# Latent attention in one DiT-like step: value products of head pairs in two column halves, four slots, maxima two items ahead

## The chip, the cores and the metric

The kernel runs on one core of a Trainium2 chip. The metric is the device time of one execution in microseconds; three runs give the time before. A NeuronCore has TensorE (PE, matrix products into PSUM; its weight loads are listed apart as PEld), VectorE (DVE), ScalarE (ACT), GpSimd (POOL) and SyncE (SP), each with an instruction stream of its own that runs in order, tied together by semaphores.

## What is computed

One inference step of a two-layer backbone over 128 context tokens and 512 latent tokens. Layer 0 has differential attention, layer 1 multi-head latent attention (MLA), and each layer ends in an expert-retrieval mixer, which takes most of the time. The change touches only the attention proper of layer 1, which is, cut to what matters:

```python
MLA_HEADS = 16; MLA_QK_DIM = 96; MLA_V_DIM = 64      # SEQ 128, DEC_SEQ 512, PAST_LEN 128

def attend(q, k, v, mix):                            # in blocks of Q_BLOCK = 128 queries
    scale = Dq ** -0.5
    def one(qblk):
        s = jnp.einsum('bqhd,bkhd->bhqk', qblk, k, preferred_element_type=jnp.float32) * scale
        w = mix(jax.nn.softmax(s, axis=-1))
        return jnp.einsum('bhqk,bkhd->bqhd', w.astype(v.dtype), v)

op = mla_out(qp, kp, vp, mla_wo[j])                               # 128 context queries, 128 context keys
os_ = mla_out(qs, jnp.concatenate([k_lat, k_ctx], axis=1),        # 512 latent queries,
              jnp.concatenate([v_lat, v_ctx], axis=1), mla_wo[j]) # 512 latent + 128 cached keys
```

with `mix` the identity. All is float32.

## The kernel before

The kernel is one program of blocks with a barrier of all engines between them; in a block, each engine has its instructions written out by hand, and semaphores count finished instructions. Layer 1 goes: norm, `mla_compress`, then for each of two groups of eight heads `mla_heads` (queries, keys, values of the group) and `mla_attention`, then the output product. `mla_attention` runs twice.

It works through 40 items in a call: a head (eight) and a block of 128 queries (five, `qb` 0 to 3 latent, 4 context). A latent item has 640 keys, a context item 128: four large items and one small for each head. The steps of an item are:

- scores on TensorE (lines 1110 and 1111, in a small item 1113): 128 queries by 512 and 128 keys, contraction over 96, into two PSUM banks of `ps`, 0 and 1 or 2 and 3 in turn;
- maximum on VectorE (line 1154) and its scaling by the query's norm (line 1157), into `small`;
- exponential on ScalarE (line 1183) from PSUM into a slot of `pr` (three slots), with the row sum, which comes as a short instruction of its own;
- reciprocal of the sum (line 1163) and the weights, `pr` times it, in place, on VectorE (line 1166);
- transposes of `pr` on TensorE (line 1123), one for each 128 keys, into banks 4 and 5, and their copy to `pT` (two slots) on ScalarE (line 1192);
- value product on TensorE (line 1134): 128 columns of `V`, which are two heads, as stationary operand, `pT` as moving one, into bank 6 or 7. Half of the result belongs to the other head and is thrown away: the copy of the result on ScalarE (line 1198) takes 64 partitions.

A float32 product is two passes of TensorE, with a weight load each, so that a value product of five matmuls shows as x10 in the trace; a transpose is one.

The order is software-pipelined by hand. TensorE in step w: scores of w, value product of w - 3, transposes of w - 2. ScalarE: exponential of w, copy of w - 2, result of w - 3. VectorE: maximum of w + 1, then weights of w. All VectorE instructions count up one semaphore, `ma_w`, so that a wait for some step of it is a wait for all before it. Before its transposes TensorE waits for the weights of that item:

```python
pe.wait_ge(sem(n_ + "w"), 4 * (o + w + 1) + (2 if w + 1 < len(items) else 0))
```

`diff_attention` of layer 0 has the same shape, with two score products for each item, one on rows 0 to 63 of the array and one on rows 64 to 127 (lines 486 and 487), value product on line 509.

Of the kernel before, what the change touches and what calls it, by code (L numbers as in the profile page):

```python
# [21 lines left out]
ALU = mybir.AluOpType  # L22
ACT = mybir.ActivationFunctionType
AX = mybir.AxisListType.X

P = 128
# [34 lines left out]
def mixed(nc, cst, inp, outs, g_dram, x_dram):  # L61
# [32 lines left out]
    def bank2(b, n=T, p=P):  # L94

        return ps[0:p, b:b + 2, :].rearrange("p a n -> p (a n)")[:, 0:n]
# [987 lines left out]

    def mla_attention(g, qT, kT, V, rsq, oT, pr, pT):

        items = [(h, qb) for h in range(GH) for qb in range(TB)]
        n_ = "ma_"
        o = g * len(items)

        def width(qb):
            return T if qb < 4 else TP

        with nc.Block() as block:
            @block.sync
            def _(sp):
                if g == 0:
                    for name in sorted(sems):
                        if name.startswith("mh_"):
                            sp.sem_clear(sems[name])  # L1100

            @block.tensor
            def _(pe):
                def scores(w):
                    h, qb = items[w]
                    q, k, b = qT[0:DQ, h, qb * P:(qb + 1) * P], kT[0:DQ, h, :], 2 * (w % 2)
                    if w >= 2:
                        pe.wait_ge(sem(n_ + "exp"), o + w - 1)
                    if qb < 4:
                        pe.matmul(ps[:, b, :], q, k[:, 0:TS], start=True, stop=True)  # L1110
                        mm = pe.matmul(ps[:, b + 1, 0:TC], q, k[:, T:TK], start=True, stop=True)
                    else:
                        mm = pe.matmul(ps[:, b, 0:TP], q, k[:, TS:T], start=True, stop=True)
                    mm.then_inc(sem(n_ + "s"), 1)

                def turns(w):
                    h, qb = items[w]
                    blocks = (0, 1, 2, 3, 5) if qb < 4 else (4,)
                    pe.wait_ge(sem(n_ + "w"), 4 * (o + w + 1) + (2 if w + 1 < len(items) else 0))
                    if w >= 1:  # L1120
                        pe.wait_ge(sem(n_ + "pT"), o + w)
                    for k in range(len(blocks)):
                        mm = pe.transpose(bank2(4)[:, k * P:(k + 1) * P], pr[:, w % 3, 0, k * P:(k + 1) * P], ident)
                    mm.then_inc(sem(n_ + "t"), 1)

                def values(w):
                    h, qb = items[w]
                    blocks = (0, 1, 2, 3, 5) if qb < 4 else (4,)
                    pe.wait_ge(sem(n_ + "pT"), o + w + 1)
                    if w >= 2:  # L1130
                        pe.wait_ge(sem(n_ + "o"), o + w - 1)
                    for k, kb in enumerate(blocks):

                        mm = pe.matmul(ps[:, 6 + w % 2, 0:P], V[:, kb, (h // 2) * P:(h // 2 + 1) * P],
                                       pT[:, w % 2, k * P:(k + 1) * P], start=k == 0, stop=k == len(blocks) - 1)
                    mm.then_inc(sem(n_ + "pv"), 1)

                for w in range(len(items) + 3):
                    if w < len(items):
                        scores(w)  # L1140
                    if w >= 3:
                        values(w - 3)
                    if 2 <= w < len(items) + 2:
                        turns(w - 2)

            @block.vector
            def _(v):
                s = sem(n_ + "w")

                def maxima(w):  # L1150
                    n = width(items[w][1])
                    z = small[:, 16 * (w % 2):16 * (w % 2) + 16]
                    v.wait_ge(sem(n_ + "s"), o + w + 1)
                    v.tensor_reduce(z[:, 0:1], bank2(2 * (w % 2), n), AX, ALU.max).then_inc(s, 1)
                    v.wait_ge(s, 4 * o + (1 if w == 0 else 4 * w - 1))
                    h, qb = items[w]
                    v.tensor_scalar(z[:, 2:3], z[:, 0:1], rsq[:, 1, qb, h:h + 1], None, ALU.mult).then_inc(s, 1)

                def weights(w):
                    n = width(items[w][1])  # L1160
                    z = small[:, 16 * (w % 2):16 * (w % 2) + 16]
                    v.wait_ge(sem(n_ + "exp"), o + w + 1)
                    v.reciprocal(z[:, 6:7], z[:, 4:5]).then_inc(s, 1)
                    v.wait_ge(s, 4 * (o + w) + 3 + (2 if w + 1 < len(items) else 0))
                    p0 = pr[:, w % 3, 0, 0:n]
                    v.tensor_scalar(p0, p0, z[:, 6:7], None, ALU.mult).then_inc(s, 1)

                maxima(0)
                for w in range(len(items)):
                    if w + 1 < len(items):  # L1170
                        maxima(w + 1)
                    weights(w)

            @block.scalar
            def _(act):
                def exps(w):
                    h, qb = items[w]
                    n = width(qb)
                    z = small[:, 16 * (w % 2):16 * (w % 2) + 16]
                    if w >= 3:  # L1180
                        act.wait_ge(sem(n_ + "t"), o + w - 2)
                    act.wait_ge(sem(n_ + "w"), 4 * o + (2 if w == 0 else 4 * w))
                    act.activation(pr[:, w % 3, 0, 0:n], bank2(2 * (w % 2), n), ACT.Exp, bias=z[:, 2:3],
                                   scale=rsq[:, 2, qb, h:h + 1], accum_out=z[:, 4:5]).then_inc(sem(n_ + "exp"), 1)

                def copies(w):
                    h, qb = items[w]
                    n = width(qb)
                    act.wait_ge(sem(n_ + "t"), o + w + 1)
                    if w >= 2:  # L1190
                        act.wait_ge(sem(n_ + "pv"), o + w - 1)
                    act.copy(pT[:, w % 2, 0:n], bank2(4, n)).then_inc(sem(n_ + "pT"), 1)

                def results(w):
                    h, qb = items[w]
                    act.wait_ge(sem(n_ + "pv"), o + w + 1)
                    r = 64 * (h % 2)
                    act.copy(oT[r:r + 64, (g * GH + h) // 2, qb * P:(qb + 1) * P], ps[r:r + 64, 6 + w % 2, 0:P])\
                       .then_inc(sem(n_ + "o"), 1)

                for w in range(len(items) + 3):
                    if w < len(items):
                        exps(w)
                    if 2 <= w < len(items) + 2:
                        copies(w - 2)
                    if w >= 3:
                        results(w - 3)
# [676 lines left out]
    with es:  # L1884
# [20 lines left out]
        with ExitStack() as st:  # L1905
# [12 lines left out]
            with ExitStack() as sa:  # L1918
                cqT = sb(sa, "cqT", [P, 4, T])
                ckvT = sb(sa, "ckvT", [P, 2, TK])  # L1920
                kpeT, kpe_sq, kpe_rot = (sb(sa, name, [DR, TK]) for name in ("kpeT", "kpe_sq", "kpe_rot"))
                cq_ms = sb(sa, "cq_ms", [P, T])
                cos, sin = sb(sa, "cos_mla", [P, TK]), sb(sa, "sin_mla", [P, TK])
                with ExitStack() as s2:
                    mla_compress(ring, cqT, ckvT, kpeT, kpe_sq, kpe_rot, cq_ms, cos, sin, sb(s2, "scr_c", [P, 6, T]),
                                 sb(s2, "abuf_c", [P, 2, 2048]), sb(s2, "acc_c", [P, 2, 2, 256]))
                qT, kT = sb(sa, "qTm", [P, GH, T]), sb(sa, "kTm", [P, GH, TK])
                V = sb(sa, "Vm", [P, 6, GH * DV])
                for g in range(2):
                    with ExitStack() as s2:  # L1930
                        mla_heads(g, ring, indT, cqT, ckvT, kpe_sq, kpe_rot, cq_ms, qT, kT, V, rsq, cos, sin,
                                  sb(s2, f"scr_m{g}", [16, 2, TK]), sb(s2, f"xk{g}", [P, 2, TK]), hT[:, 4:6, :], hT[:, 6:8, :])
                    with ExitStack() as s2:
                        mla_attention(g, qT, kT, V, rsq, hT, sb(s2, f"pr_m{g}", [P, 3, 1, T]), sb(s2, f"pT_m{g}", [P, 2, T]))
            with ExitStack() as s2:
                out_product(1, ring, hT, J_WO1, range(J_PQ[1], J_PQ[1] + 3), sb(s2, "oh1", [P, DC, T], F32R),
                            sb(s2, "ol1", [P, DC, T], F32R), sb(s2, "woh1", [P, 2, DC, P], F32R),
# [155 lines left out]
```

## Time and profile before

| | us |
|---|---|
| runs | 4040.15, 4044.76, 4044.55 |
| median | 4044.55 |
| profiled execution, span of its instructions | 4043.5 |
| first call of `mla_attention` in it | 2219.65 to 2335.54, 115.89 |
| second call | 2420.90 to 2536.80, 115.90 |

The profiled execution has no time of its own beside its span, from the first to the last instruction; it is 1.05 us below the median. A profile gives for each instruction its start and duration; rows of the timeline merge neighbours of one line (xN), and what stands in brackets is how long the engine was idle before it and who released it. "PE" durations of matmuls include the pipeline's drain, so that starts, not durations, tell the rate: the distance from one weight load to that of the next step is what a step costs TensorE.

### The profile page before, as it was taken

Reading aid. Unit: us, or ns where it says so; the run is one execution under the profiler, and the core shown is the slowest. Engines: PE = TensorE matmul, PEld = TensorE weight load, DVE = VectorE, ACT = ScalarE, POOL = GpSimd, SP = SyncE. Lnnn points to the kernel's source line nnn. Section 1 sums busy time; section 2 is a strip of 40 time slices with the busy share of each in tenths; the row PEclk is TensorE's granted clock in tenths of the full one; section 3 lists DMA queues with packets and bytes.
Section 4 is the critical chain, followed back from the end, with each engine's and each line's share of the span. In section 5 each row is a group of like instructions: output and inputs, shape, how many; then the busy total and the mean of one; then the engine's idle time right before and its main releaser. Section 6 shows DMA issues by size and latency. Waiting matters only on the chain. (4 is left out here: it accounts for less than half of the span.)

```text
span 4043.5 us, 55694 instructions
## 1 busy us (share of the span) xinstructions
PE 3793.5 (94%) x20589; PEld 3188.6 (79%) x20589; DVE 3269.8 (81%) x6832; ACT 1769.0 (44%) x2928; POOL 988.0 (24%) x796
## 2 busy tenths in 40 slices
PE   6999999978999999999989898897789999999999
PEld 3555789677999999999854646896779999999998
DVE  2755648987999999999863525389979999999998
ACT  2324622185444444444423545322854444444443
POOL 0000000074333333333200000000743333333332
PEclk8999989999999999999989999898999999999999
DMA  6320020269999999999741010200799999999997
GB/s 238 136 94 11 22 89 37 98 174 361 420 419 414 405 403 404 404 404 406 312 177 43 1 42 1 109 37 22 185 375 420 417 412 407 405 405 405 405 406 300
DMA packets 268125, 1033.69 MB, mean 256 GB/s; under 512 B 147056, under 2 KB 150064, under 8 KB 159920
## 3 DMA queue, kind: packets, MB, share of 16 engines
q0 software_dynamic: 77184, 562.07, 34.7%
q1 hardware_dynamic: 190672, 468.07, 30.4%
q8 instruction: 164, 2.69, 0.3%
q14 instruction: 105, 0.86, 0.1%
HBM read 970.69 MB, written 59.39 MB: 255 GB/s over the span
## 5 line engine op out<-in xcount | busy, mean ns | idle before, releaser
L1637 POOL DMA_INDIRECT gbuf<-in_uv,rows x340 | 514.5, 1513 | 866.3 <-DVE hT L1821 796.5
L1429 POOL TENSOR_SCALAR pqT<-iota,selT 128x128 f32<-128x128 f32 x256 | 203.4, 809 | 1337.4 <-ACT selT L1371 1300.9
L1821 DVE SCALAR_TENSOR_TENSOR hT<-gbuf,act,hT 128x1024 f32<-128x1024 f32 x336 | 416.9, 1282 | 6.0
L1806 DVE SCALAR_TENSOR_TENSOR gbuf<-gbuf,ht 128x1024 f32<-128x1024 f32 x340 | 402.3, 1220 | 10.7 <-DMA gbuf<-in_uv,rows 10.7
L1637 POOL DMA_INDIRECT xT<-in_uv,rows x172 | 256.9, 1493 | 471.0 <-DVE hT L1821 392.9
L1653 PE MATMUL ps<-h1h,U1h 128*128 128x384 f32 x1024 | 344.5, 336 | 7.7 <-DVE U1l L1780 7.6
L1653 PE MATMUL ps<-h0h,U0h 128*128 128x384 f32 x1024 | 344.7, 337 | 5.1 <-DVE U0l L1780 5.1
L1653 PE MATMUL ps<-h0h,U0l 128*128 128x384 f32 x1024 | 344.2, 336 | 0.0
L1653 PE MATMUL ps<-h0l,U0h 128*128 128x384 f32 x1024 | 343.9, 336 | 0.0
L1653 PE MATMUL ps<-h1h,U1l 128*128 128x384 f32 x1024 | 343.9, 336 | 0.0
L1653 PE MATMUL ps<-h1l,U1h 128*128 128x384 f32 x1024 | 343.5, 335 | 0.0
L1726 ACT ACTIVATE ring<-ps 128x384 f32<-128x384 f32 x256 | 125.9, 492 | 379.0 <-PE ps L1653 378.9
L1736 ACT ACTIVATE act<-act 128x2 f32<-128x2 f32 x256 | 51.8, 202 | 457.1 <-DVE gbuf L1806 300.3
L1318 PE MATMUL ps<-pqT,w 128*128 128x128 f32 x1536 | 192.1, 284 | 50.8 <-DVE w L1562 36.1
L1268 PE MATMUL ps<-hT,ring 128*128 128x128 f32 x1920 | 231.7, 281 | 6.1 <-ACT hT L258 4.5
L1268 PEld LDWEIGHTS ps<-hT,ring 128*128 128x128 f32 x1920 | 224.3, 196 | 10.7 <-ACT hT L258 5.7
L1318 PEld LDWEIGHTS ps<-pqT,w 128*128 128x128 f32 x1536 | 181.7, 197 | 61.4 <-DVE w L1562 31.7
L1806 DVE SCALAR_TENSOR_TENSOR xT<-xT,ht 128x1024 f32<-128x1024 f32 x172 | 203.7, 1220 | 9.8 <-DMA xT<-in_uv,rows 9.8
L1821 DVE SCALAR_TENSOR_TENSOR hT<-xT,act,hT 128x1024 f32<-128x1024 f32 x168 | 208.4, 1282 | 3.0
L1653 PEld LDWEIGHTS ps<-h1h,U1h 128*128 128x128 f32 x1024 | 193.0, 189 | 11.1 <-DVE U1l L1780 8.7
L1653 PEld LDWEIGHTS ps<-h0h,U0h 128*128 128x128 f32 x1024 | 193.3, 189 | 8.2 <-DVE U0l L1780 5.8
L101 PE MATMUL ps<-hT,ring 128*128 128x512 f32 (+1 forms) x368 | 195.1, 613 | 4.5 <-ACT hT L258 4.5
(379 smaller groups left out, 9053.6 us busy)
## 6 DMA issues: line engine op xcount, KB each, us to landing
ring<-in_u SPq DMA_DIRECT2D x128, 1024.0 KB, 13.4
ring<-in_v SPq DMA_DIRECT2D x128, 1024.0 KB, 9.4
ring<-in_wts SPq DMA_DIRECT2D x26, 2048.0 KB, 8.3
gates<-ring SPq DMA_DIRECT2D x32, 1536.0 KB, 8.5
ring<-gates SPq DMA_DIRECT2D x64, 768.0 KB, 16.4
abuf<-in_ada_mid POOLq DMA_DIRECT2D x16, 1024.0 KB, 5.1
xT<-in_ada_late SPq DMA_DIRECT2D x16, 1024.0 KB, 4.8
abuf_c<-in_ada_late POOLq DMA_DIRECT2D x8, 1024.0 KB, 5.1
```

The costliest lines, as they stand in the source:

```text
L101: e.matmul(out[:, 0:512], lhsT, rhs[:, 0:512], start=start, stop=stop)
L1268: mm = pe.matmul(ps[:, 5 + n % 3, q * P:(q + 1) * P], w[:, dc, q * P:(q + 1) * P], hT[:, dc, tb * P:(tb + 1) * P], start=dc == 0, stop=dc ...
L1318: mm = pe.matmul(ps[:, b + t // 4, (t % 4) * P:(t % 4 + 1) * P], one1[:, r % 2, t, :], one2[:, r % 2, t, :], start=True, stop=True)
L1429: last = pool.tensor_scalar(one2[:, r % 2, t, :], iota[:], selT[:, 1, t0 + t:t0 + t + 1], selT[:, 2, t0 + t:t0 + t + 1], ALU.is_equal, ALU ...
L1637: pool.indirect_dma_start(out=slots[m % GSLOTS], out_offset=None, in_=inp[f"uv{l}"], in_offset=bass.IndirectOffsetOnAxis(ap=rows[:, c:c + ...
L1653: mm = pe.matmul(up_bank(k), Us[x][:, k, dc * P:(dc + 1) * P], hs[y][:, dc, :], start=dc == 0 and x + y == 0, stop=dc == DC - 1 and x == 1)
L1726: act.activation(Wf[:, k, :], up_bank(k), ACT.Gelu_apprx_tanh).then_inc(sem(n_ + "gelu"), 1)
L1736: act.activation(act4[:, n % 2, 0:2], act4[:, n % 2, 0:2], ACT.Gelu_apprx_tanh)\
L1806: v.scalar_tensor_tensor(u, u, 1.0, ht[:, m // P, :], ALU.mult, ALU.mult, accum_out=act4[:, n % 2, m % 2:m % 2 + 1]).then_inc(sem(n_ + "do ...
L1821: v.scalar_tensor_tensor(y, x, w, y, ALU.mult, ALU.add).then_inc(sem(n_ + "acc"), 1)
```

## The change

Items now come in pairs: `(pair, qb, c)`, with c the head of the pair, so that items 2u and 2u + 1 are the same query block of two neighbouring heads, and large and small items come eight and two. The value product is one for a pair (`values(u)`): for each block of keys one matmul with the 64 columns of the first head into partitions 0 to 63 of the bank, one with those of the second head into partitions 64 to 127. The number of matmuls is as before, each half as wide. One copy of 128 partitions takes the result of a pair. `pr` and `pT` have four slots each; `pT` lies in `hT[:, 4:8]` in the first call and in `cqT` in the second, both free there. `small` has four sets of columns. VectorE takes two maxima first and then goes on with the maximum of i + 2 and the weights of i. TensorE in step i: scores of i, in odd steps the value product of the pair (i - 5, i - 4), transposes of i - 2. ScalarE: exponential of i, copy of i - 2, in odd steps the result of a pair.

```diff
-        items = [(h, qb) for h in range(GH) for qb in range(TB)]
+        items = [(2 * pair + c, qb) for pair in range(GH // 2) for qb in range(TB) for c in range(2)]
+        def scaled(i):
+            return 4 * o + (2 * i + 2 if i < 2 else 4 * i - 2)
+        def weighed(i):
+            return 4 * o + (4 * i + 8 if i < N - 2 else 2 * N + 2 * i + 2)
...
-                    pe.wait_ge(sem(n_ + "w"), 4 * (o + w + 1) + (2 if w + 1 < len(items) else 0))
-                    if w >= 1:
-                        pe.wait_ge(sem(n_ + "pT"), o + w)
...
-                        mm = pe.matmul(ps[:, 6 + w % 2, 0:P], V[:, kb, (h // 2) * P:(h // 2 + 1) * P],
-                                       pT[:, w % 2, k * P:(k + 1) * P], start=k == 0, stop=k == len(blocks) - 1)
+                def turns(i):
+                    pe.wait_ge(sem(n_ + "w"), weighed(i))
+                    if i >= 1:
+                        pe.wait_ge(sem(n_ + "pT"), o + i)
+                    for k in range(width(i) // P):
+                        mm = pe.transpose(bank2(4)[:, k * P:(k + 1) * P], pr[:, i % 4, k * P:(k + 1) * P], ident)
...
+                def values(u):
...
+                    pe.wait_ge(sem(n_ + "pT"), o + 2 * u + 2)
+                    if u >= 2:
+                        pe.wait_ge(sem(n_ + "o"), ou + u - 1)
                     for k, kb in enumerate(blocks):
+                        for c in range(2):
+                            h = items[2 * u + c][0]
+                            mm = pe.matmul(ps[DV * c:DV * (c + 1), 6 + u % 2, 0:P], V[:, kb, h * DV:(h + 1) * DV],
+                                           pT[:, (2 * u + c) % 4, k * P:(k + 1) * P], start=k == 0, stop=k == len(blocks) - 1)
...
-                for w in range(len(items) + 3):
-                    if w < len(items):
-                        scores(w)
-                    if w >= 3:
-                        values(w - 3)
-                    if 2 <= w < len(items) + 2:
-                        turns(w - 2)
+                for i in range(N + 5):
+                    if i < N:
+                        scores(i)
+                    if i >= 5 and i % 2:
+                        values((i - 5) // 2)
+                    if 2 <= i < N + 2:
+                        turns(i - 2)
...
                 maxima(0)
-                for w in range(len(items)):
-                    if w + 1 < len(items):
-                        maxima(w + 1)
-                    weights(w)
+                maxima(1)
+                for i in range(N):
+                    if i + 2 < N:
+                        maxima(i + 2)
+                    weights(i)
...
-                    act.copy(oT[r:r + 64, (g * GH + h) // 2, qb * P:(qb + 1) * P], ps[r:r + 64, 6 + w % 2, 0:P])\
+                    act.copy(oT[:, (g * GH + h) // 2, qb * P:(qb + 1) * P], ps[:, 6 + u % 2, 0:P]).then_inc(sem(n_ + "o"), 1)
...
-                        mla_attention(g, qT, kT, V, rsq, hT, sb(s2, f"pr_m{g}", [P, 3, 1, T]), sb(s2, f"pT_m{g}", [P, 2, T]))
+                        mla_attention(g, qT, kT, V, rsq, hT, sb(s2, f"pr_m{g}", [P, 4, T]), (hT[:, 4:8, :], cqT)[g])
```

What it moves shows in the order of the instructions. VectorE at the start of a call, before: a reduction (`TENSOR_REDUCE`) is a maximum, the two instructions with `pr_m` and the `RECIPROCAL` are the weights.

```order
L1154 TENSOR_REDUCE small<-ps 128x1 [waits ma_s]
L1157 TENSOR_SCALAR small<-small,rsq 128x1 [waits ma_w]
L1154 TENSOR_REDUCE small<-ps 128x1 [waits ma_s]
L1157 TENSOR_SCALAR small<-small,rsq 128x1 [waits ma_w]
L1163 RECIPROCAL small<-small 128x1 [waits ma_exp]
L1166 TENSOR_SCALAR pr_m<-pr_m,small 128x640 [waits ma_w]
L1154 TENSOR_REDUCE small<-ps 128x1 [waits ma_s]
L1157 TENSOR_SCALAR small<-small,rsq 128x1 [waits ma_w]
```

VectorE at the same place in the changed kernel:

```order
L1167 TENSOR_REDUCE small<-ps 128x1 [waits ma_s]
L1169 TENSOR_SCALAR small<-small,rsq 128x1 [waits ma_w]
L1167 TENSOR_REDUCE small<-ps 128x1 [waits ma_s]
L1169 TENSOR_SCALAR small<-small,rsq 128x1 [waits ma_w]
L1167 TENSOR_REDUCE small<-ps 128x1 [waits ma_s]
L1169 TENSOR_SCALAR small<-small,rsq 128x1 [waits ma_w]
L1174 RECIPROCAL small<-small 128x1 [waits ma_exp]
L1176 TENSOR_SCALAR pr_m<-pr_m,small 128x640 [waits ma_w]
```

The maximum of item 2 has moved from behind the weights of item 0 to ahead of them, and so on for each later item.

TensorE in the second head of a call, before: scores on lines 1110 and 1111, value product on line 1134, transposes on line 1123.

```order
L1110 MATMUL ps<-kTm,qTm 128x512 [waits ma_exp]
L1111 MATMUL ps<-kTm,qTm 128x128
L1134 MATMUL ps<-pT_m,Vm 128x128 [waits ma_o,ma_pT]
L1134 MATMUL ps<-pT_m,Vm 128x128 x4
L1123 MATMUL ps<-consts,pr_m 128x128 [waits ma_pT,ma_w]
L1123 MATMUL ps<-consts,pr_m 128x128 x4
```

TensorE in two consecutive steps of the changed kernel, an even and an odd one: scores on lines 1122 and 1123, transposes on line 1133, value product on line 1145, `hT` its slots for `pT`.

```order
L1122 MATMUL ps<-kTm,qTm 128x512 [waits ma_exp]
L1123 MATMUL ps<-kTm,qTm 128x128
L1133 MATMUL ps<-consts,pr_m 128x128 [waits ma_pT,ma_w]
L1133 MATMUL ps<-consts,pr_m 128x128 x4
L1122 MATMUL ps<-kTm,qTm 128x512 [waits ma_exp]
L1123 MATMUL ps<-kTm,qTm 128x128
L1145 MATMUL ps<-hT,Vm 64x128 [waits ma_pT]
L1145 MATMUL ps<-hT,Vm 64x128 x9
L1133 MATMUL ps<-consts,pr_m 128x128 [waits ma_pT,ma_w]
L1133 MATMUL ps<-consts,pr_m 128x128 x4
```

The value product has gone out of every second step, and has ten matmuls of 64 columns in the others; scores of i and transposes of i - 2 stand where they stood.

## Rows read from the trace of the kernel before

**Rows 1.** The page: busy time of each engine.

```profile
PE 3793.5 (94%) x20589; PEld 3188.6 (79%) x20589; DVE 3269.8 (81%) x6832; ACT 1769.0 (44%) x2928; POOL 988.0 (24%) x796
```

**Rows 2.** By stage: length; PE, PEld, DVE, ACT, POOL busy; granted clock; DMA; GB/s.

```profile
2219.65:2335.54 115.89, 99.72 (x648) 78.91 (x648) 60.12 (x160) 67.06 (x161) 0.00 (x0) 1.00 0.00 1
...
2420.90:2536.80 115.90, 99.73 (x648) 78.91 (x648) 60.14 (x160) 67.04 (x161) 0.00 (x0) 1.00 0.00 1
```

**Rows 3.** Waits in 2219 to 2330: who for whom, us, times, longest.

```profile
DVE small L1154 <- PE ps L1111: 38.3, 23, 5.7
...
PEld ps L1134 <- ACT pT_m L1192: 17.2, 23, 1.3
```

**Rows 4.** Timeline of the second head: start, duration, engine, line, operation.

```profile
2231.64 0.30 PEld L1110 LDWEIGHTS ps<-kTm,qTm 96*128 96x128 f32 x2
...
2232.62 0.19 PEld L1111 LDWEIGHTS ps<-kTm,qTm 96*128 96x128 f32 x1 [0.24 <-issue]
2232.73 1.20 PEld L1134 LDWEIGHTS ps<-pT_m,Vm 128*128 128x128 f32 x10
...
2233.84 0.58 PEld L1123 LDWEIGHTS ps<-consts,pr_m 128*128 128x128 f32 x5
...
2233.95 0.71 PE L1123 MATMUL ps<-consts,pr_m 128*128 128x128 f32 x5
...
2234.39 0.30 PEld L1110 LDWEIGHTS ps<-kTm,qTm 96*128 96x128 f32 x2
...
2235.78 0.82 DVE L1154 TENSOR_REDUCE small<-ps 128x1 f32<-128x640 f32 x1 [1.28 <-PE ps L1111]
...
2236.64 0.21 DVE L1157 TENSOR_SCALAR small<-small,rsq 128x1 f32<-128x1 f32 x1
...
2236.96 0.55 DVE L1166 TENSOR_SCALAR pr_m<-pr_m,small 128x640 f32<-128x640 f32 x1
...
2240.48 0.68 ACT L1192 COPY pT_m<-ps 128x640 f32<-128x640 f32 x1
...
2241.21 1.19 PEld L1134 LDWEIGHTS ps<-pT_m,Vm 128*128 128x128 f32 x10 [1.15 <-ACT pT_m L1192]
...
2245.58 0.30 PEld L1110 LDWEIGHTS ps<-kTm,qTm 96*128 96x128 f32 x2
```

**Rows 5.** Timeline, the small item 4: scores, maximum, scaling, weights.

```profile
2228.93 0.30 PEld L1113 LDWEIGHTS ps<-kTm,qTm 96*128 96x128 f32 x2
...
2229.47 0.29 DVE L1154 TENSOR_REDUCE small<-ps 128x1 f32<-128x128 f32 x1 [1.54 <-PE ps L1113]
2229.79 0.21 DVE L1157 TENSOR_SCALAR small<-small,rsq 128x1 f32<-128x1 f32 x1
...
2234.22 0.29 DVE L1166 TENSOR_SCALAR pr_m<-pr_m,small 128x128 f32<-128x128 f32 x1
```

**Rows 6.** Timeline, the first call: scores of item 2 and of item 39.

```profile
2223.17 1.13 PE L1110 MATMUL ps<-kTm,qTm 96*128 96x512 f32 x2 [1.10 <-ACT pr_m L1183]
...
2326.43 0.30 PEld L1113 LDWEIGHTS ps<-kTm,qTm 96*128 96x128 f32 x2
```

**Rows 7.** Timeline of differential attention, weight loads: two score products, then values.

```profile
440.83 0.29 PEld L486 LDWEIGHTS ps<-kT,qT 64*128 64x128 f32 x2 [0.63 <-ACT pr_da L572]
...
443.03 1.19 PEld L509 LDWEIGHTS ps<-pT_da,V 128*128 128x128 f32 x10
...
447.77 0.31 PEld L486 LDWEIGHTS ps<-kT,qT 64*128 64x128 f32 x4 [0.17 <-issue]
...
448.74 0.20 PEld L487 LDWEIGHTS ps<-kT,qT 64*128 64x128 f32 x2 [0.23 <-issue]
449.06 1.19 PEld L509 LDWEIGHTS ps<-pT_da,V 128*128 128x128 f32 x10
```

**Rows 8.** Timeline, start of differential attention: first scores, idle before in brackets.

```profile
337.46 1.14 PE L486 MATMUL ps<-kT,qT 64*128 64x512 f32 x4 [2.20 <-PEq L267]
```

**Rows 9.** By stage, columns as in rows 2: just after those scores.

```profile
339.00:340.00 1.00, 0.00 (x0) 0.00 (x0) 0.96 (x3) 0.00 (x0) 0.00 (x0) 0.50 0.27 75
```

More of the change, by code:

```diff
@@ L1085, in mla_attention, with width, scores_at @@
     def mla_attention(g, qT, kT, V, rsq, oT, pr, pT):
-        items = [(h, qb) for h in range(GH) for qb in range(TB)]
+        items = [(2 * pair + c, qb) for pair in range(GH // 2) for qb in range(TB) for c in range(2)]
         n_ = "ma_"
-        o = g * len(items)
-        def width(qb):
-            return T if qb < 4 else TP
+        N = len(items)
+        o, ou = g * N, g * N // 2
+        def width(i):
+            return T if items[i][1] < 4 else TP
+        def scaled(i):
+            return 4 * o + (2 * i + 2 if i < 2 else 4 * i - 2)
+        def weighed(i):
+            return 4 * o + (4 * i + 8 if i < N - 2 else 2 * N + 2 * i + 2)
+        def scores_at(i):
+            return bank2(2 * (i % 2), width(i))
         with nc.Block() as block:
@@ L1103, in _, with scores @@
             def _(pe):
[L1104 to L1108, printed above, removed]
+                def scores(i):
+                    h, qb = items[i]
+                    q, k, b = qT[0:DQ, h, qb * P:(qb + 1) * P], kT[0:DQ, h, :], 2 * (i % 2)
+                    if i >= 2:
+                        pe.wait_ge(sem(n_ + "exp"), o + i - 1)
                     if qb < 4:
@@ L1114, in scores @@
                     mm.then_inc(sem(n_ + "s"), 1)
-                def turns(w):
-                    h, qb = items[w]
-                    blocks = (0, 1, 2, 3, 5) if qb < 4 else (4,)
-                    pe.wait_ge(sem(n_ + "w"), 4 * (o + w + 1) + (2 if w + 1 < len(items) else 0))
-                    if w >= 1:
-                        pe.wait_ge(sem(n_ + "pT"), o + w)
-                    for k in range(len(blocks)):
-                        mm = pe.transpose(bank2(4)[:, k * P:(k + 1) * P], pr[:, w % 3, 0, k * P:(k + 1) * P], ident)
-                    mm.then_inc(sem(n_ + "t"), 1)
@@ L1126, in values @@
[L1126 to L1131, printed above, removed]
+                def turns(i):
[4 more added lines that the diff above has]
+                        mm = pe.transpose(bank2(4)[:, k * P:(k + 1) * P], pr[:, i % 4, k * P:(k + 1) * P], ident)
+                    mm.then_inc(sem(n_ + "t"), 1)
@@ L1132, in values @@
+                def values(u):
+                    qb = items[2 * u][1]
+                    blocks = (0, 1, 2, 3, 5) if qb < 4 else (4,)
+                    pe.wait_ge(sem(n_ + "pT"), o + 2 * u + 2)
+                    if u >= 2:
+                        pe.wait_ge(sem(n_ + "o"), ou + u - 1)
                     for k, kb in enumerate(blocks):
-                        mm = pe.matmul(ps[:, 6 + w % 2, 0:P], V[:, kb, (h // 2) * P:(h // 2 + 1) * P],
-                                       pT[:, w % 2, k * P:(k + 1) * P], start=k == 0, stop=k == len(blocks) - 1)
+                        for c in range(2):
+                            h = items[2 * u + c][0]
+                            mm = pe.matmul(ps[DV * c:DV * (c + 1), 6 + u % 2, 0:P], V[:, kb, h * DV:(h + 1) * DV],
+                                           pT[:, (2 * u + c) % 4, k * P:(k + 1) * P], start=k == 0, stop=k == len(blocks) - 1)
@@ L1148, in _, with z_ @@
                 s = sem(n_ + "w")
[L1150 to L1156, printed above, removed]
+                def z_(i):
+                    return small[:, 16 * (i % 4):16 * (i % 4) + 16]
@@ L1157, in maxima, with weights @@
+                def maxima(i):
+                    (h, qb), z = items[i], z_(i)
+                    v.wait_ge(sem(n_ + "s"), o + i + 1)
+                    v.tensor_reduce(z[:, 0:1], scores_at(i), AX, ALU.max).then_inc(s, 1)
+                    v.wait_ge(s, scaled(i) - 1)
                     v.tensor_scalar(z[:, 2:3], z[:, 0:1], rsq[:, 1, qb, h:h + 1], None, ALU.mult).then_inc(s, 1)
[L1159 to L1162, printed above, removed]
+                def weights(i):
+                    z, p0 = z_(i), pr[:, i % 4, 0:width(i)]
+                    v.wait_ge(sem(n_ + "exp"), o + i + 1)
@@ L1163, in weights @@
                     v.reciprocal(z[:, 6:7], z[:, 4:5]).then_inc(s, 1)
-                    v.wait_ge(s, 4 * (o + w) + 3 + (2 if w + 1 < len(items) else 0))
-                    p0 = pr[:, w % 3, 0, 0:n]
+                    v.wait_ge(s, weighed(i) - 1)
                     v.tensor_scalar(p0, p0, z[:, 6:7], None, ALU.mult).then_inc(s, 1)
                 maxima(0)
-                for w in range(len(items)):
-                    if w + 1 < len(items):
-                        maxima(w + 1)
-                    weights(w)
+                maxima(1)
@@ L1174, in _ @@
+                for i in range(N):
+                    if i + 2 < N:
+                        maxima(i + 2)
+                    weights(i)
             @block.scalar
             def _(act):
[L1176 to L1183, printed above, removed]
-                                   scale=rsq[:, 2, qb, h:h + 1], accum_out=z[:, 4:5]).then_inc(sem(n_ + "exp"), 1)
@@ L1186, in copies @@
[L1186 to L1197, printed above, removed]
-                    act.copy(oT[r:r + 64, (g * GH + h) // 2, qb * P:(qb + 1) * P], ps[r:r + 64, 6 + w % 2, 0:P])\
-                       .then_inc(sem(n_ + "o"), 1)
@@ L1201, in _, with exps @@
[L1201 to L1207, printed above, removed]
+                def exps(i):
+                    h, qb = items[i]
+                    z = small[:, 16 * (i % 4):16 * (i % 4) + 16]
+                    if i >= 4:
+                        act.wait_ge(sem(n_ + "t"), o + i - 3)
+                    act.wait_ge(sem(n_ + "w"), scaled(i))
+                    act.activation(pr[:, i % 4, 0:width(i)], scores_at(i), ACT.Exp, bias=z[:, 2:3],
+                                   scale=rsq[:, 2, qb, h:h + 1], accum_out=z[:, 4:5]).then_inc(sem(n_ + "exp"), 1)
@@ new lines, in copies, with results @@
+                def copies(i):
+                    act.wait_ge(sem(n_ + "t"), o + i + 1)
+                    if i >= 4:
+                        act.wait_ge(sem(n_ + "pv"), ou + i // 2 - 1)
+                    act.copy(pT[:, i % 4, 0:width(i)], bank2(4, width(i))).then_inc(sem(n_ + "pT"), 1)
+                def results(u):
+                    h, qb = items[2 * u]
+                    act.wait_ge(sem(n_ + "pv"), ou + u + 1)
+                    act.copy(oT[:, (g * GH + h) // 2, qb * P:(qb + 1) * P], ps[:, 6 + u % 2, 0:P]).then_inc(sem(n_ + "o"), 1)
@@ L1210, in expert_choice @@
+                for i in range(N + 5):
+                    if i < N:
+                        exps(i)
+                    if 2 <= i < N + 2:
+                        copies(i - 2)
+                    if i >= 5 and i % 2:
+                        results((i - 5) // 2)
     def expert_choice(l, w3, pqT, keysT, selT, rows, gates, steps, sc, s2, cand, c2, vals, idxu, posu, idxp, ranks, posh,
```

## The prediction

> **What bounds the kernel now.** The page of the whole execution comes first: TensorE is busy for 94% of the span [rows 1]. That says little about this change, since it touches only the two calls of `mla_attention`. The table by stage shows them: two stretches of 115.89 and 115.90 us, alike to 0.01 us, in which TensorE is busy for 86%, VectorE for 52% and ScalarE for 58%, at a granted clock of 1.00 [rows 2]. So the change plays on 232 us of 4043.5, and nothing outside these stretches changes: the same chunks are loaded in the neighbouring blocks and all stages are separated by barriers.
>
> I call the steps of one item S (scores), M (maximum and its scaling), E (exponential), W (reciprocal and weights), T (transposes), C (copy of the transposed weights), V (value product) and R (copy of the result). Waits inside the stretch [rows 3]: VectorE waits 38.3 us for scores, which costs nothing, as it has time to spare; the weight loads of V wait 17.2 us for C. The timeline shows how the work turns [rows 4]. On TensorE a large S takes 1.09 us (2231.64 to 2232.73), V 1.11 (2232.73 to 2233.84), T 0.55 (2233.84 to 2234.39), in all 2.75 us. A small item (a fifth of them) has 0.22, 0.22 and 0.11: two, two and one pass of 128 rows, at the 0.11 us that each of V's ten takes. Five items, one head, would be 4 x 2.75 + 0.55 = 11.55 us; from one head to the next it is 13.94 (2231.64 to 2245.58). The 2.4 us between are waits of V for C, as before the V at 2241.21. So TensorE binds, with holes. What keeps W out of this is one step of slack: T of item i-2 waits for W of item i-2, and VectorE wrote that right behind M of item i-1, whose scores came a whole step earlier.
>
> **The change: what it removes.** If the two 64-column halves run side by side, ten V matmuls of a pair take what five did, about 1.11 us instead of 2.22. The trace has no column halves. It has row halves: in differential attention the two score products use rows 0 to 63 and 64 to 127. Where the second has to wait its turn, both take 2.20 us (440.83 to 443.03); where both are ready, 1.29 us (447.77 to 449.06) [rows 7]. So disjoint tiles do overlap, and I take 1.11 us for a pair, with 0.2 us at each change of shape: V's first load starts 0.32 us after the last one of such scores (448.74 and 449.06), where in the latent attention it is 0.11 (2232.62 and 2232.73). The other end is no overlap, 2.2 us. The Trainium skill, "TensorEngine Tiling (Array Packing)", section "Key Properties", says that tiles work independently of one another but that a change of tiling mode drains TensorE. By the first V is halved, as I take it; by the second each pair pays for two switches. No run here shows that for columns. A drain would have to take over 0.49 us, (3.17 - 1.09 - 1.11) / 2, to lengthen the odd steps; the rows show 0.2.
> R copies 128 partitions once instead of 64 twice, and four slots free E and C from waits; both lie on ScalarE, which is at 58% [rows 2], and are worth nothing on the path.
>
> **What it adds.** The order of instructions shows it. TensorE still issues S(i), then V in every second step, then T(i-2). But VectorE now writes M(i) ahead of W(i-2), and M(i) needs S(i). So T(i-2) waits for W(i-2), that for M(i), that for S(i), all within one step; and S(i+1) stands behind T(i-2) on TensorE. No slack is left: S, M, W and T follow each other in a ring, once per item. Behind the waiting T stand on TensorE S(i+1) and all the rest, behind M(i) on VectorE stands W(i-2), and ScalarE's C(i-2) waits for T. The price of one turn, from [rows 4]: start of S to start of M 1.39 us (2234.39 to 2235.78); M to scaling 0.86; scaling to the weights 0.32 (2236.64 to 2236.96); weights 0.55; from an engine's end to the weight load that waited 0.05 (C at 2240.48 ends 2241.16, V loads at 2241.21); T 0.55. Sum 3.72 us, where TensorE alone needs 2.75. V of the odd steps goes from 1.09 to about 2.6 of these 3.72 us and the T it precedes is not ready until 3.17, so it is hidden.
> Steps with a small item, from [rows 5]: with large S and small W and T, 1.39 + 0.86 + 0.32 + 0.29 + 0.05 + 0.11 = 3.02; with small S and large W and T, 0.54 (2228.93 to 2229.47) + 0.32 + 0.32 + 0.55 + 0.05 + 0.55 = 2.33. Ten steps hold six of the first, two and two of the others: 22.32 + 6.04 + 4.66 = 33.02 us. Before, ten items (two heads) take 27.87. **The change costs 5.15 us per ten items.**
> ScalarE keeps up: E 0.98 with its read of the sum, C 0.69 and half an R are under 2 us of 3.72. S(i+1) needs E(i-1), which started 2.6 us into the step before and is over.
>
> **The sum for one call.** Fill: S(2) starts 3.52 us after S(0) (2219.65 to 2223.17, [rows 6]), as now, as it hangs on the first E. Then six steps of 3.72 and two of 2.33 bring S(10) to 30.50, three rounds of 33.02 bring S(40) to 129.56, so S(39) would start at 127.23. Now it starts at 106.78 (2326.43). The tail: before, 9.11 us (2326.43 to 2335.54). After, T(37) is ready at 1.8, C(37) is done at 3.3 (T's end 0.82 after its first load, from 2233.84 to 2234.66, then 0.69), then T(38), V(18), T(39), C(39), V(19) and R, about 0.1 + 1.4 + 0.6 + 0.3 + 0.5 + 0.3, 6.5 in all. So 127.23 + 6.5 = 133.7 us instead of 115.9, or 17.8 more, twice: **35.7 us**. The profiled span is 4043.5 us and the median of the runs 4044.55, 1 us above. 4044.55 + 35.7 = 4080 us.
>
> **Rivals.** *The halves do not overlap* (the change does not do what it says). V takes 2.2 us and 0.4 for the switches: an odd large step is 1.09 + 2.6 + 0.55 = 4.24 (+0.52), the odd one with small T 3.80 (+0.78), the odd one with small S 3.37 (+1.04). Ten steps get 2.86 us longer, a call about 11.8, in all 23.5 on top: 4104 us. Against it stand [rows 7]; for it, that these are rows and not columns.
> *The clock falls.* In the even steps TensorE idles for 1.8 us of 3.72 (S is over by 1.39, T is ready at 3.17). At the start of the first call it idled for 1.10 us (the release of S(2), [rows 6]) with the clock at 1.00 [rows 2]; at the start of differential attention, after an idle of 2.20 us and a short burst, the granted clock fell to 0.50, the level of 1.2 GHz [rows 8, 9]. 1.8 lies between. At 1.2 GHz throughout, S adds 1.07 us and T 0.55: large steps 5.34, the others 4.20 and 3.10, ten 46.6, or 13.6 us more, 109 in all, and V peeks out for another 16: 4205 us. A third of the time low would give 4120.
> *Faster.* If W(i-2) were ready when S(i) ends, the ring would not close and TensorE would be the bound: ten items need 8 x 1.09 + 0.44 of S, 4.4 + 0.22 of T, and 4 x 1.5 + 0.6 of V, 20.4 us instead of 27.9, 60 us less in all, 3985 us. The ring decides as soon as M(i) stands ahead of W(i-2) on VectorE, which waits in order; the rows of the order say that it does, in all steps but the last two. So hardly likely. The same for no change: the ring's surplus would have to be below 0.1 us a step, where it is 0.5.
>
> **How the numbers follow.** Ring with V hidden: 0.57, 4072 to 4088 (0.1 us either way in each of 80 steps). No overlap, wholly or in part: 0.20, 4088 to 4106. Clock low for part of the time: 0.15, 4095 to 4205, near its lower end. Faster 0.05; no change 0.03. A measurement of this kernel can tell about 0.2%, or 8 us, from no change. Leaving out the faster case and the long tail of the clock, the range is 4068 to 4118. Chances: faster 0.05, within 0.2% 0.03, slower 0.92.
>
> **What would show it.** In the profile of the changed kernel each call should be 134 us; VectorE's W should start 0.32 us after the scaling of the item two ahead; the waits should name weight loads of T waiting for VectorE's weights, some 1.8 us in even and 0.5 us in odd steps, 80 to 100 us in all; V's weight loads should wait for nothing. V of a pair at 1.1 to 1.3 us means that the halves overlap, 2.2 that they do not. Granted clock 1.00 in both stretches. I am wrong if T does not wait for VectorE, or if a large step is 2.7 us or shorter.

## The result: slower, and by twice the forecast

The changed kernel takes 4116.4 us (median of 4 runs, 4111.75 to 4125.3), the kernel before in the same comparison 4044.66 us: a ratio of 1.0182, 95% interval 1.0168 to 1.0196, 71.7 us more. The forecast was slower, 4080 us with a range to 4118; the median lies inside that range, but only just, and the move of 71.7 us is twice the 35.7 us of the forecast: one term of its sum is missing.

The table by stage of the changed kernel puts all of it into the two calls (length; PE, PEld, DVE, ACT, POOL busy; granted clock; DMA; GB/s):

```profile
2217.99:2368.42 150.43, 107.52 (x648) 73.11 (x648) 60.04 (x160) 64.02 (x141) 0.00 (x0) 0.82 0.00 1
2368.42:2453.75 85.33, 81.12 (x245) 35.48 (x245) 23.08 (x24) 34.00 (x39) 0.00 (x0) 0.98 0.14 50
2453.75:2607.36 153.61, 111.24 (x648) 75.80 (x648) 60.03 (x160) 64.15 (x141) 0.00 (x0) 0.80 0.00 1
```

150.43 and 153.61 us stand where 115.89 and 115.90 were [rows 2]: 72.2 us more, and the span grew from 4043.5 to 4115.6, by 72.1. What lies between the calls is as long as it was, 85.33 against 85.36 us. Two things are new in these rows. The calls are longer, and the granted clock in them is 0.82 and 0.80, where it was 1.00.

The waits in the first call of the changed kernel (who for whom: us in total, times, longest):

```profile
DVE small L1167 <- PE ps L1123: 78.7, 31, 5.7
ACT pr_m L1193 <- DVE small L1174: 53.9, 32, 2.6
PEld ps L1133 <- DVE pr_m L1176: 49.4, 35, 2.1
```

The third has no counterpart in the same view of the kernel before: the weight loads of the transposes T wait for VectorE's weights W, 35 times in 40 items. The wait of the value product V for its copy, 17.2 us there [rows 3], has shrunk to one of 0.5 us.

The timeline (start, duration, engine, line, operation) of one large even step at full clock: scores S, maximum M, its scaling, weights W, transposes T, next scores:

```profile
2239.63 0.30 PEld L1122 LDWEIGHTS ps<-kTm,qTm 96*128 96x128 f32 x2
...
2241.02 0.82 DVE L1167 TENSOR_REDUCE small<-ps 128x1 f32<-128x640 f32 x1 [1.94 <-PE ps L1123]
...
2241.88 0.21 DVE L1169 TENSOR_SCALAR small<-small,rsq 128x1 f32<-128x1 f32 x1
...
2242.20 0.55 DVE L1176 TENSOR_SCALAR pr_m<-pr_m,small 128x640 f32<-128x640 f32 x1
2242.81 0.53 PEld L1133 LDWEIGHTS ps<-consts,pr_m 128*128 128x128 f32 x5 [2.02 <-DVE pr_m L1176]
...
2243.30 0.30 PEld L1122 LDWEIGHTS ps<-kTm,qTm 96*128 96x128 f32 x2
```

That is the ring, link by link: 1.39 from S to M, 0.86 to the scaling, 0.32 to the weights, 0.61 to T, 0.49 to the next S, 3.67 us in all. The forecast had 3.72. The odd step behind it:

```profile
2244.58 1.07 PEld L1145 LDWEIGHTS ps<-hT,Vm 128*64 128x64 f32 x20
...
2246.48 0.53 PEld L1133 LDWEIGHTS ps<-consts,pr_m 128*128 128x128 f32 x5 [0.82 <-DVE pr_m L1176]
...
2246.97 0.30 PEld L1125 LDWEIGHTS ps<-kTm,qTm 96*128 96x128 f32 x2
```

From 2243.30 to 2246.97 it is 3.67 us again. All twenty weight loads of a pair's value product start within 1.07 us: the halves do overlap, and it gains nothing, since T is not ready for another 0.82 us.

And the step just before these two, an odd one, when the clock was low:

```profile
2233.85 0.93 PEld L1133 LDWEIGHTS ps<-consts,pr_m 128*128 128x128 f32 x5 [2.12 <-DVE pr_m L1176]
...
2234.76 0.55 PEld L1122 LDWEIGHTS ps<-kTm,qTm 96*128 96x128 f32 x2
...
2237.35 0.82 DVE L1167 TENSOR_REDUCE small<-ps 128x1 f32<-128x640 f32 x1 [3.56 <-PE ps L1123]
...
2239.14 0.53 PEld L1133 LDWEIGHTS ps<-consts,pr_m 128*128 128x128 f32 x5 [0.33 <-DVE pr_m L1176]
```

From T to T it is 5.29 us (2233.85 to 2239.14) instead of 3.67. S to M takes 2.59 instead of 1.39, T to S 0.91 instead of 0.49; VectorE's part is the same. TensorE is in the ring twice, and at 1.2 GHz both of its links are nearly twice as long (1.9 times).

When does the clock fall? In both calls for the first time near the end of the first hole between S and T, in a step that has no value product yet (PE's view; the clock falls at about 2224.6):

```profile
2224.68 1.33 PE L1133 MATMUL ps<-consts,pr_m 128*128 128x128 f32 x5 [1.83 <-DVE pr_m L1176]
```

After it the clock rises and falls again, 10 falls in the first call and 13 in the second, and is low for 55 and 61 us. It does not fall at each hole: from 2321 to 2337 it holds over three, of 1.29, 1.56 and 1.83 us.

### The profile page after: what moved, and what is told of

The parts are those of the page before. It is cut to its first block and busy times, and to the rows that moved or that the text cites. A ratio compares the mean times of both kernels' runs of the same rounds, so it can differ in the third digit from the quotient of the medians.

```text
span 4115.6 us, 55608 instructions
## 1 busy us (share of the span) xinstructions
PE 3816.3 (93%) x20589; PEld 3181.1 (77%) x20589; DVE 3269.5 (79%) x6832; ACT 1763.1 (43%) x2888; POOL 987.7 (24%) x796
## 5 line engine op out<-in xcount | busy, mean ns | idle before, releaser
L1167 DVE TENSOR_REDUCE small<-ps 128x1 f32<-128x640 f32 (+1 forms) x80 | 57.4, 718 | 179.3 <-PE ps L1123 161.3
```

What stands on the lines that cost most here:

```text
L1167: v.tensor_reduce(z[:, 0:1], scores_at(i), AX, ALU.max).then_inc(s, 1)
```

## Experiments

Two theories had to be told from the rivals: that the missing slack (T of i - 2 behind M of i) makes the ring, and that the rest is the clock, which falls because TensorE is idle in the ring. The rivals: the halves or the switches of shape cost the time, or a longer wait that has nothing to do with the clock.

### Maxima one item ahead, all else as changed

```diff
                 maxima(0)
-                maxima(1)
                 for i in range(N):
-                    if i + 2 < N:
-                        maxima(i + 2)
+                    if i + 1 < N:
+                        maxima(i + 1)
                     weights(i)
```

(`scaled` and `weighed`, the counts that others wait for, follow the new order.)

> The changed kernel with one thing undone: VectorE again takes the maximum only one item ahead (M of i + 1, then W of i); pairs, column halves and four slots stay. Theory of the ring (T of i - 2 waits for W of i - 2, that for M of i, that for S of i): the ring opens, no step waits for VectorE, and TensorE is the bound with 18.4 us for ten items (8 x 1.09 + 0.44 of S, 4.4 + 0.22 of T, 4 x 1.09 + 0.22 of V), a call 80 to 95 us, the kernel 3985 to 4005 us. Rival, the halves or the order in pairs cost the time (switches of shape, clock): no better than 4080 us, and T still does not wait for VectorE.

Measured: 3999.63 us, ratio 0.9891 to the kernel before, interval 0.9875 to 0.9908. Stages, the two calls:

```profile
2218.97:2310.61 91.64, 82.43 (x648) 58.44 (x648) 59.59 (x160) 61.01 (x141) 0.00 (x0) 1.00 0.00 1
...
2395.90:2487.70 91.80, 82.39 (x648) 58.41 (x648) 59.59 (x160) 61.11 (x141) 0.00 (x0) 1.00 0.00 1
```

The ring is open, though not every wait is gone: weight loads of T still wait for VectorE in this call, 11 us in all, against 49 in the changed kernel. One order on VectorE is worth 117 us of 4116. The pairs, the halves and the slots are no fault: with them and the old order of maxima a call takes 91.7 us instead of 115.9. This is also the fastest version found.

### The kernel before, maxima two items ahead

```diff
                 maxima(0)
-                for w in range(len(items)):
-                    if w + 1 < len(items):
-                        maxima(w + 1)
+                maxima(1)
+                for w in range(N):
+                    if w + 2 < N:
+                        maxima(w + 2)
                     weights(w)
```

(with the same two functions of counts as in the change, and four sets of columns in `small`.)

> The kernel before with one thing done: maxima two items ahead (with four sets of columns in small); item order, 128-column value products in every step and three slots stay. Theory of the ring: a large step takes 3.67 us as in the changed kernel; V of 1.11 us lies in every hole, so that TensorE idles 0.9 us a step and not 1.75; a call of 131 to 134 us. If the idle of 1.75 us is what lowers the clock, it stays at 1.00 here and the kernel takes 4075 to 4082 us. If the ring by itself lowers it, 4100 to 4120. Rival, the halves are to blame: within 5 us of the kernel before, 4045.

Measured: 4096.3 us, ratio 1.0133 (1.0116 to 1.0150), 52 us slower than the kernel before. Stages, and one large step of its timeline:

```profile
2216.25:2357.43 141.18, 108.03 (x648) 83.62 (x648) 60.07 (x160) 68.60 (x161) 0.00 (x0) 0.95 0.00 1
2444.36:2585.00 140.64, 106.87 (x648) 82.29 (x648) 60.08 (x160) 68.63 (x161) 0.00 (x0) 0.96 0.00 1
```

```profile
2248.65 0.30 PEld L1117 LDWEIGHTS ps<-kTm,qTm 96*128 96x128 f32 x2
...
2249.73 1.20 PEld L1141 LDWEIGHTS ps<-pT_m,Vm 128*128 128x128 f32 x10
2251.82 0.53 PEld L1130 LDWEIGHTS ps<-consts,pr_m 128*128 128x128 f32 x5 [0.90 <-DVE pr_m L1173]
2252.32 0.30 PEld L1117 LDWEIGHTS ps<-kTm,qTm 96*128 96x128 f32 x2
```

The ring alone, without a single half product, gives the step of 3.67 us (2248.65 to 2252.32) and the wait of 0.90 that was expected. The time fits neither of the two cases that were written down: it is 14 us above the end of the one in which the clock holds, and 4 below the start of the other. Part of it is the old item order: one head takes 16.69 us (2235.63 to 2252.32), so two take 33.4, where the pairs take 32.55 (the next run, 2242.97 to 2275.52), as its small step is 2.71 us, V waiting 0.75 for its copy. Part is the clock, 0.95 and 0.96 and not 1.00. It falls twice in each call. The first fall stands at the start, around the end of the same hole of 1.83 us without a value product as in the changed kernel. The second stands behind a small item, where V is short (start, duration, engine, line; PE's view):

```profile
2323.28 0.39 PE L1141 MATMUL ps<-pT_m,Vm 128*128 128x128 f32 x2
2325.26 1.33 PE L1130 MATMUL ps<-consts,pr_m 128*128 128x128 f32 x5 [1.60 <-DVE pr_m L1173]
2326.38 1.92 PE L1117 MATMUL ps<-kTm,qTm 96*128 96x512 f32 x2
```

The five transposes take 1.33 us where they take 0.77 at full clock (the row at 2318.62 of the same view), and the scores 1.92 instead of 1.02. That hole, 1.60 us here, comes once a head, and the clock stays at 1.00 over most of them; in the changed kernel a hole of 1.3 to 1.8 us stands in every even step.

### Work added in the even steps

```diff
+                    if 2 <= i < N and i % 2 == 0:
+                        pe.wait_ge(sem(n_ + "exp"), o + i)
+                        for k in range(5):
+                            pe.matmul(ps[:, 2 * ((i + 1) % 2), 0:P], kT[0:DQ, 0, 0:P], kT[0:DQ, 1, 0:P], start=True, stop=True)
                     if 2 <= i < N + 2:
                         turns(i - 2)
```

The products go into the bank that the next scores overwrite.

> The changed kernel with work added and nothing taken away: in each even step from 2 to 38, TensorE makes five float32 products of 128 x 128 (ten passes, 1.1 us at full clock) that nobody reads, between S and T, where it now idles for 1.75 us. Theory that 41 of the 72 us are the clock: the granted clock is 0.97 or more in both calls, each takes 131 to 134 us, the kernel 4074 to 4082, faster than the changed kernel with less to do. Rival, the time is not the clock's but that of a longer wait: 4116 or more.

Measured: 4080.69 us, ratio 1.0085 (1.0068 to 1.0102), with 190 more matmul passes in each call 36 us faster than the changed kernel without them. Stages:

```profile
2217.90:2349.70 131.80, 106.57 (x838) 79.80 (x838) 60.10 (x160) 63.97 (x141) 0.00 (x0) 1.00 0.00 1
2436.55:2568.30 131.75, 106.57 (x838) 79.79 (x838) 60.07 (x160) 63.95 (x141) 0.00 (x0) 1.00 0.00 1
```

This separates the two parts. 131.8 us is a call of the ring at full clock: 15.9 more than 115.9, 31.8 for both. The changed kernel's two calls are 304.0 us, 40.5 more than these 263.6: that is what the clock takes. The rival of a wait that the clock has no part in falls. The added products leave the ring's own steps as they are: five steps around the small items take 14.17 us here (2242.97 to 2257.14, start of T to start of T), and 14.17 in the changed kernel where its clock is high:

```profile
2322.08 0.53 PEld L1133 LDWEIGHTS ps<-consts,pr_m 128*128 128x128 f32 x5 [0.82 <-DVE pr_m L1176]
...
2336.25 0.53 PEld L1133 LDWEIGHTS ps<-consts,pr_m 128*128 128x128 f32 x5 [2.02 <-DVE pr_m L1176]
```

One hole of the full length is left open in this run, in the third step of a call, where there is neither a value product yet nor an added one (PE's view):

```profile
2228.27 0.77 PE L1133 MATMUL ps<-consts,pr_m 128*128 128x128 f32 x5 [1.83 <-DVE pr_m L1180]
```

The clock holds over it, so one idle stretch of 1.83 us is not enough by itself to lower the clock.

### Value product and its copy one step later, in the kernel before

```diff
-                    if w >= 3:
-                        values(w - 3)
+                    if w >= 4:
+                        values(w - 4)
...
-                    act.copy(pT[:, w % 2, 0:n], bank2(4, n)).then_inc(sem(n_ + "pT"), 1)
+                    act.copy(pT[:, w % 4, 0:n], bank2(4, n)).then_inc(sem(n_ + "pT"), 1)
```

(the copy of the result and the waits on the value product as much later; the four slots lie where the change puts them.)

> The kernel before with the value product and the copy of its result one step later (V of w - 4, four slots for the transposed weights); item order, 128-column products and maxima one ahead stay. If the wait of V for C (2.4 us in each head) is what separates a call from TensorE's own 11.55 us a head, a call falls from 115.9 to 96 to 100 us and the kernel to 4005 to 4015 us. If another wait comes in its place (T for C of the item before, E for M), 4025 to 4045. Against the run with maxima one ahead it tells what the halves bring and what the slots.

Measured: 4019.23 us, ratio 0.9939 (0.9923 to 0.9956). Stage of the first call:

```profile
2218.80:2321.50 102.70, 95.38 (x648) 77.50 (x648) 60.10 (x160) 65.63 (x161) 0.00 (x0) 1.00 0.00 1
```

A call takes 13.2 us less than before, where 16 to 20 were expected, and the kernel's time lies 4 us above the range of that case. The wait of V for C is what separated the kernel before from TensorE's own work, for the most part; in its place T now waits for VectorE behind the small items:

```profile
2251.39 1.20 PEld L1134 LDWEIGHTS ps<-hT,Vm 128*128 128x128 f32 x10
...
2253.42 0.53 PEld L1123 LDWEIGHTS ps<-consts,pr_m 128*128 128x128 f32 x5 [0.83 <-DVE small L1163]
```

So of the 44 us between the kernel before and the run with maxima one ahead, 25 come from the slack of one step and the slots for it. The other 20 come from the halves together with the order in pairs; the next run tells these two apart.

### The halves in turn, maxima one ahead

```diff
-                    for k, kb in enumerate(blocks):
-                        for c in range(2):
+                    for c in range(2):
+                        for k, kb in enumerate(blocks):
```

> The run with maxima one ahead, 3999.6 us, with the two halves of a value product in turn: the five blocks of the first head, then the five of the second, the same ten matmuls of 64 columns. Theory that the halves overlap because neighbours in the queue use disjoint columns: V of a pair goes from 1.07 to 2.1 or 2.3 us, TensorE needs about 22.7 us for ten items, a call 100 to 106 us instead of 91.7, the kernel 4016 to 4030 us, no better than the value products of 128 columns with the same slack (4019). Rival, TensorE finds the overlap whatever the order: 3998 to 4003.

Measured: 4021.56 us, ratio 0.9944 (0.9926 to 0.9962); calls of 101.40 and 101.39 us at a clock of 1.00:

```profile
2219.10:2320.50 101.40, 92.15 (x648) 69.52 (x648) 58.83 (x160) 62.15 (x141) 0.00 (x0) 1.00 0.00 1
```

The same matmuls in another order cost 9.7 us a call, 22 us in all, and leave no gain over products of 128 columns. So without the overlap the pairs and the narrower products bring nothing, and the 20 us above are the gain of the overlap. One value product of each of the two runs, with the transposes behind it; first alternating, then in turn:

```profile
2256.55 0.19 PEld L1123 LDWEIGHTS ps<-kTm,qTm 96*128 96x128 f32 x1 [0.24 <-issue]
2256.86 1.07 PEld L1145 LDWEIGHTS ps<-hT,Vm 128*64 128x64 f32 x20
...
2258.10 0.53 PEld L1133 LDWEIGHTS ps<-consts,pr_m 128*128 128x128 f32 x5 [0.17 <-DVE small L1169]
```

```profile
2240.06 1.78 PEld L1145 LDWEIGHTS ps<-hT,Vm 128*64 128x64 f32 x20
2242.01 0.53 PEld L1133 LDWEIGHTS ps<-consts,pr_m 128*128 128x128 f32 x5 [0.17 <-issue]
```

1.24 against 1.95 us from the first load to T. In turn is less than the 2.22 of two full products. The last load of a large S starts 0.31 us before the first of V (0.32 at 2254.32 in the run in turn), where it was 0.11 us with products of 128 columns [rows 4]: the 0.2 us for a change of shape.

### The halves in turn, in the changed kernel

The edit is the swap of the two loops from the run above, applied to the changed kernel.

> The changed kernel, ring and all, with the halves of a value product in turn. V should go to 2.2 us and fill all of the odd steps' hole, a large odd step 3.9 instead of 3.67 us, so 4 us more a call at full clock: without the clock 4082 to 4088 us. If idle TensorE lowers the clock, fewer and shorter stretches at the low level than in the changed kernel, 4090 to 4112 in all, less than 4116 with no work taken away. Rival, the clock goes by the even steps' idle alone: 4120 to 4130.

Measured: 4119.9 us, ratio 1.0196 (1.0177 to 1.0214). Stages:

```profile
2216.50:2368.42 151.92, 111.59 (x648) 80.48 (x648) 60.05 (x160) 64.25 (x141) 0.00 (x0) 0.87 0.00 1
2458.74:2610.10 151.36, 110.73 (x648) 81.08 (x648) 60.02 (x160) 64.25 (x141) 0.00 (x0) 0.89 0.00 1
```

My figure was missed and the rival's range only just. The time is that of the changed kernel: the intervals of the two ratios overlap, and the two calls take 303.3 us where they took 304.0. But it is made up otherwise. At full clock the longer V costs what was expected, 4 us a call. A large odd step is 3.72 us (2244.16 to 2247.88 from T to T) and hides it; around the small items it shows, 2.86 us (2285.30 to 2288.16) instead of 2.28, and ten steps take 33.54 us (2264.55 to 2298.09) instead of 32.55. Added to the 263.6 us of the run with unread products that makes 271.6, and leaves 31.7 us for the clock instead of 40.5 (an estimate, as no run has these calls at full clock throughout). The clock is indeed low for less time and falls less often, 14 times instead of 23: by the means of 0.87 and 0.89 for about 73 us of the two calls, by those of 0.82 and 0.80 for about 116. So filling the odd steps' hole helps the clock in part and does not hold it up; filling the even ones' did.

### Transposes one step later, maxima two ahead

```diff
-                    if i >= 5 and i % 2:
-                        values((i - 5) // 2)
-                    if 2 <= i < N + 2:
-                        turns(i - 2)
+                    if i >= 7 and i % 2:
+                        values((i - 7) // 2)
+                    if 3 <= i < N + 3:
+                        turns(i - 3)
```

(and the copies on ScalarE as much later.)

> The changed kernel with maxima two ahead kept, but transposes and their copy one step later (T of i - 3) and the value product and its copy two steps later (pair i - 7, i - 6), as four slots allow. Theory that the missing slack is the fault and not the distance of the maxima: T waits for W of an item whose M came a step before, the ring opens, TensorE binds, a call 85 to 97 us, the kernel 3990 to 4010 us, clock 1.00. Rival, maxima ahead of weights delay W itself so that the wait stays: a call over 110 us, 4040 or more.

Measured: 4000.8 us, ratio 0.9902 (0.9883 to 0.9921); both calls as this first one:

```profile
2219.10:2313.30 94.20, 82.65 (x648) 58.44 (x648) 59.69 (x160) 61.05 (x141) 0.00 (x0) 1.00 0.00 1
```

Maxima two ahead are all but harmless when the transposes go one step back as well: a call is 2.5 us longer than with maxima one ahead, the kernel the same within its noise. The fault of the change is that it moved one of them and not the other.

## Why the prediction was right about the ring and wrong about the clock

- *What bounds the kernel now*: right. TensorE with holes, V waiting for C. The run with values one step later took most of the holes away and gained 13.2 us a call, of the 2.4 us a head, 19 a call, that I had counted.
- *The ring*: right, and each link is in the trace. 3.67 us a large step against 3.72, 2.28 for a small one (2249.25 to 2251.53 in the changed kernel) against 2.33, a call at full clock 131.8 against 133.7. T after a wait costs 0.49 us, not 0.55. The term was 35.7 us for two calls; 31.8 was measured, where the clock was held.
- *V hidden, halves overlapping*: right. 1.07 us of loads where 1.11 was taken. The rival without overlap was priced too high: it gave V 2.2 us and 0.4 for the switches and 2.86 us more for ten items, and in turn V takes 1.95 with its switch and ten steps 1.0 us more, as most of it hides in the ring. What I did not see is that the overlap hangs on the order in the queue.
- *The clock*: the step that failed. The sum of 35.7 us held no term for it. The prediction said "1.8 lies between", between an idle of 1.10 us at which the clock had held and one of 2.20 us after which it had fallen, and gave the clock 0.15. It fell in both calls, 0.82 and 0.80 on the mean, and cost 40.5 us, more than the ring itself. The case was priced from 4095 to 4205, "near its lower end", and a third of the time low at 4120; measured were 36 and 40% of the calls low, and 4116. So the mechanism was among the rivals with the right price and far too small a chance. The idle itself was worked out rightly, 1.8 us, and 1.82 was measured. What was wrong was to place it by its length between two single gaps. In the run with unread products one hole of 1.83 us stands alone in each call and the clock holds over it. In the six calls where the holes follow each other (both calls of the changed kernel, of the run with maxima two ahead only, and of the run with the ring and the halves in turn) the first fall stands within 0.4 us of the end of the first hole of 1.83 us, behind idle stretches of 0.93 and 1.09 us at the start of the call. The ring repeats the hole in every even step for 150 us, and the clock fell 23 times in the two calls. The runs do not say why it falls at some of the later holes and not at others.
- *The sum*: 35.7 forecast; 31.8 (ring) + 40.5 (clock) = 72.3 measured, against 71.7 in the medians. The range ended at 4118 and held the time by 2 us; that is luck. 4118 is merely where the prediction broke off the clock's case, and two calls like the second one, 3.2 us longer than the first, would have given about 4119.6 (an estimate).
- *Faster* did not occur, and its price was fair: opening the ring, which was its condition, gives 4000, where 3985 was worked out.

## What to carry to other kernels

Count the steps between an instruction's producer and its consumer on every engine's queue before moving one of them: taking a step ahead on one in-order engine pushes everything behind it on that engine back, and slack of one step can vanish in a ring through two engines. When a change makes TensorE idle in every step, give the clock a term in the sum: here a hole of 1.8 us in every second step cost more than the ring that made it. Weigh that case by how often the hole repeats, not by its length alone: one of 1.83 us by itself did not lower the clock, holes of 1.60 us once a head did so once a call, and holes of 1.3 to 1.8 us in every second step some ten times. A cheap test is to put unused products into the gap: if the kernel gets faster and the granted clock rises, it was the clock.

## What the runs showed of the hardware

- Products into disjoint column halves (64 columns each) run side by side if they alternate in the queue: ten of float32, 128 rows moving, from the first load to the next shape in 1.24 us; in turn 1.95. Both include about 0.2 us for the change of shape; the distance from the last load of S to the first of V is 0.31 us with halves and 0.11 with 128 columns [rows 4].
- The granted clock of TensorE fell to 0.50 (1.2 GHz) 10 and 13 times in calls of 150.4 and 153.6 us in which TensorE was idle (PE's view) for up to 1.83 us between S and T in every second step and for 0.58 us in most of the others. It stayed at 1.00 for 131.8 us with these holes filled down to 0.71 by 1.1 us of unread products, and with one open hole of 1.83 us near the start. It fell twice in each call of 141 us (0.95 and 0.96) with 1.83 us once at the start, 0.71 us in most steps and 1.60 once a head. With the odd holes filled and the even ones open it was low for 73 us of two calls instead of 116. The work was the same 648 passes a call in all but the one with unread products. Added work made a kernel 36 us faster.
